# Half of a step's value products issued ahead of the second head's transposes, in grouped and latent attention

## The reference

```python
def sink_attend(q, segments, sink):          # grouped: 16 query heads of 64, 4 key heads, window 128
    s = jnp.einsum('bqhgd,bkhd->bhgqk', q, k) * WIN_SCALE      # masked outside the window
    p = jax.nn.softmax(jnp.concatenate(scores + [sink_col], axis=-1), axis=-1)
    outs.append(jnp.einsum('bhgqk,bkhd->bqhgd', p[..., start:start + n], v))

def mla_attend(q_nope, q_rope, k_nope, k_rope, v):             # latent: 8 heads of 128 + 64
    s = (jnp.einsum('bqhd,bkhd->bhqk', q_nope, k_nope) + jnp.einsum('bqhr,bkr->bhqk', q_rope, k_rope)) * MLA_SCALE
    p = jax.nn.softmax(s, axis=-1)
    return jnp.einsum('bhqk,bkhd->bqhd', p, v)
```

## Time and profile before

| | us |
|---|---|
| runs of the kernel before | 2820.78, 2811.59, 2815.4; median 2815.4 |
| profiled execution, its own time | 2812.94 |
| its span, first to last instruction | 2811.3 |
| PE busy | 2719.0 (97%) |
| DVE, ACT, POOL busy | 1747.4 (62%), 1250.4 (44%), 232.2 (8%) |
| grouped attention, layer 0 | 785 to 949 of the span |
| latent attention, layer 0 | 1070 to 1161 |
| grouped attention, layer 1 | 2301 to 2393 |
| latent attention, layer 1 | 2485 to 2530 |
| PE's granted clock over the span | 0.99 of full speed |

### The profile page before, as it was taken

One profiled execution on the slowest core, in us unless ns is written; L12 is line 12 of the kernel. 1 busy time (PEld: TensorE's weight loads), 2 busy tenths in 40 slices (PEclk: granted clock), 3 DMA queues, 4 the chain that ended last, 5 costly groups with the idle time before them and its releaser, 6 DMA issues.

```text
span 2811.3 us, 42833 instructions
## 1 busy us (share of the span) xinstructions
PE 2719.0 (97%) x15754; PEld 2282.3 (81%) x15754; DVE 1747.4 (62%) x2898; ACT 1250.4 (44%) x2228; POOL 232.2 (8%) x318
## 2 busy tenths in 40 slices
PE   8999999999899999999999999999999989998998
PEld 6888898876666776788888898888988677877998
DVE  7777376656755443367676386773777776636764
ACT  3222354336555434445223363223553566554444
POOL 0000010110100000010000000000102110001000
PEclk9999999999999999999999999999999999999999
DMA  7555366420111221145554455553665222414654
GB/s 280 181 200 182 93 178 227 136 90 31 53 38 46 68 88 37 60 157 184 167 188 155 128 175 175 198 183 94 179 197 186 84 76 76 143 58 150 238 172 136
DMA packets 106596, 385.49 MB, mean 137 GB/s; under 512 B 11985, under 2 KB 13281, under 8 KB 104529
## 3 DMA queue, kind: packets, MB, share of 16 engines
q1 hardware_dynamic: 86018, 303.34, 33.4%
q0 software_dynamic: 20432, 80.18, 8.7%
HBM read 379.27 MB, written 4.20 MB: 136 GB/s over the span
## 4 chain that ended last, share of the span: by engine, by line
PE 86%; DVE 8%; ACT 3%; issue 2%; DMA 1%; POOL 0%; SPq 0%; POOLq 0%; DVEq 0%; ACTq 0%
PE ps L1982 24%; PE ps L1983 23%; PE ps L1990 23%; PE ps L921 3%; PE ps L900 3%; PE ps L883 2%; DVE wlo L1494 2%; PE ps L2046 1%; PE ps L2048 1%; PE ps L2043 1%; PE ps L873 1%; DVE mx L771 1%; ACT prob L687 1%; PE ps L1922 1%; PE ps L879 1%
## 5 line engine op out<-in xcount | busy, mean ns | idle before, releaser
L1494 DVE TENSOR_TENSOR wlo<-raw,whi 128x1024 fp32r<-128x1024 f32 x572 | 698.0, 1228 | 436.2 <-ACT whi L1181 435.5
L1982 PE MATMUL ps<-xhi,whi 128*128 128x512 f32 (+1 forms) x2432 | 823.9, 353 | 9.7 <-DVE xlo L1685 9.6
L1181 ACT ACTIVATE whi<-raw 128x1024 fp32r<-128x1024 f32 x572 | 604.8, 1058 | 487.9 <-PE ps L1990 443.6
L1983 PE MATMUL ps<-xlo,whi 128*128 128x512 f32 (+1 forms) x2432 | 815.4, 349 | 0.0
L1982 PEld LDWEIGHTS ps<-xhi,whi 128*128 128x128 f32 x2432 | 464.2, 191 | 75.5 <-issue 8.8
L1983 PEld LDWEIGHTS ps<-xlo,whi 128*128 128x128 f32 x2432 | 464.5, 191 | 57.3
L1990 PE MATMUL ps<-xhi,wlo 128*128 128x512 f32 (+1 forms) x2432 | 506.8, 351 | 1.6 <-DVE wlo L1494 1.6
L1990 PEld LDWEIGHTS ps<-xhi,wlo 128*128 128x128 f32 x2432 | 400.9, 191 | 59.5 <-DVE wlo L1494 2.3
L1752 DVE SCALAR_TENSOR_TENSOR work<-ada,work 128x1024 f32<-128x1024 f32 x256 | 299.8, 1221 | 4.6 <-DMA ada<-in_ada_rows 4.6
L1982 PE MATMUL ps<-ghi,whi 128*128 128x256 f32 (+1 forms) x968 | 279.4, 314 | 1.9 <-ACT whi L1181 1.9
L1983 PE MATMUL ps<-glo,whi 128*128 128x256 f32 (+1 forms) x968 | 278.6, 315 | 0.0
(11 more groups left out here) (217 smaller groups left out, 3295.6 us busy)
## 6 DMA issues: line engine op xcount, KB each, us to landing
raw<-in_ffn_in SPq DMA_DIRECT2D x192, 512.0 KB, 4.8
ada<-in_ada_rows POOLq DMA_DIRECT2D x128, 512.0 KB, 4.4
raw<-in_merge SPq DMA_DIRECT2D x96, 512.0 KB, 3.6
raw<-in_ffn_out SPq DMA_DIRECT2D x88, 512.0 KB, 3.6
raw<-in_ffn_out SPq DMA_DIRECT2D x44, 384.0 KB, 3.2
raw<-in_v_a SPq DMA_DIRECT2D x32, 512.0 KB, 4.4
raw<-in_qk_a SPq DMA_DIRECT2D x32, 512.0 KB, 3.7
raw<-in_wo SPq DMA_DIRECT2D x24, 512.0 KB, 4.2
```

The costliest lines, as they stand in the source:

```text
L1181: act.activation(whi[:, g.ring(SPLIT), :], raw[:, g.ring(RAW), :], ACT.Copy).then_inc(hi_ready, 1)
L1494: dve.tensor_tensor(wlo[:, g.ring(SPLIT), :], raw[:, g.ring(RAW), :], whi[:, g.ring(SPLIT), :].bitcast(F32), ALU.subtract).then_inc(lo_rea ...
L1982: pe.matmul(o, w, hi[:, first + c, ph.span], start=start, stop=False)
L1983: pe.matmul(o, w, lo[:, first + c, ph.span], start=False, stop=False)
```

## The change

`weighted` gets an argument `part`, which takes the first or the second half of the unit's list of products, and only the second bumps the semaphore `pv`. In `b` a half is half of the key blocks with both heads, in `c` it is one head. In the second slot of a step, the first half now stands between the scores and the second head's transposes, the second half behind them. The first step has no products, and the last unit's are whole as before.

```diff
@@ -900,7 +900,7 @@
-            def weighted(u):
+            def weighted(u, part=None):
                 b, kc0 = units[u][0], first_key(ph, u)
                 pe.wait_ge(done["pt"], base(ph, "pt") + many * (u + 1))
                 if u % ph.per_block == 0:
@@ -909,6 +909,8 @@
                 pieces = [(n, kc) for n in range(many) for kc in range(kc0, T // P)]
                 if ph.mode == "b":
                     pieces = [(n, kc) for kc in range(kc0, T // P) for n in range(many)]
+                if part is not None:
+                    pieces = pieces[part * len(pieces) // 2:(part + 1) * len(pieces) // 2]
                 for n, kc in pieces:
@@ -919,7 +921,8 @@
                         last = pe.matmul(ps[rows, OUT, to:to + P], a, w, start=kc == kc0, stop=kc == T // P - 1)
-                last.then_inc(done["pv"], 1)
+                if part != 0:
+                    last.then_inc(done["pv"], 1)
@@ -942,9 +945,13 @@
                 yield
                 if s + 3 < len(units):
                     scores(s + 3)
-                if many == 2 and s < len(units):
+                if many == 2 and 1 <= s < len(units):
+                    weighted(s - 1, 0)
                     turn(s, 1)
-                if 1 <= s <= len(units):
+                    weighted(s - 1, 1)
+                elif many == 2 and s == 0:
+                    turn(s, 1)
+                elif 1 <= s <= len(units):
                     weighted(s - 1)
```

## The result

The changed kernel takes **2827.28 us**, the median of 6 runs (2822.88 to 2827.94), against 2813.82 (2811.59 to 2820.78, 6 runs) for the kernel before on the same chip: ratio 1.0041, 95% interval 1.0029 to 1.0052. By that ratio it is slower by 11.5 us (8 to 15); the two medians differ by 13.5. The profiled execution took 2827.14 us, its span 2825.5. All lines of `weighted` are L923 in it, the half weight group is L1997.

The account below looks back on a forecast made before the run. PE, with work in 97% of the span, was taken as the bound; cuts 6.9, entries 2.8, latent cuts 0.5 and new waits 4.8 less gain 6.0 made +9.0 us, 2824.4 on the median of 2815.4; range 2816 to 2833.

Parts of the forecast that it names:

- Cuts: Grouped stages: cutting a unit's value products in two costs 0.15 us each, 46 units, 6.9 us.
- Entries: Grouped stages: going from scores or masks into value products costs 0.09 us, about 31 times, 2.8 us.
- New waits: First transposes of the next step wait for the copy that half the products no longer cover: 4.8 us, latent 0.5 included.
- Gain: All four stages: waits before the second head's transposes filled by half the products, 6.0 us, of which latent 1.5.
- Latent: Latent stages of both layers: 22 cuts cost 0.5 us, new waits 0.5, waits gone give 1.5.
- idle before the second transposes: Grouped stages, outside the first step: PE's idle there falls from about 7 to 4 us.
- Entries are free: Value products behind scores do not pay the fixed part again: +1.6 us, 2817; chance 0.25.
- Every change of mode pays in full: Mask-to-product changes cost 0.2 us, half-row scores into products the fixed 0.16 again: +14.6 us, 2830; chance 0.15.
- ACT falls behind: Grouped steps: exponentials queued behind the later second copy delay the next step's transposes, 5.5 us more, 2830; chance 0.10.
- All waits gone: No cost of cuts, no new wait, every second-head wait after the first step ended: about -9 us, 2806; chance 0.05.

Follow-up runs that it names:

- second series: The changed kernel once more, no edit, against the kernel before: 2824.5 us, median of 12, ratio 1.0028 (1.0017 to 1.0039).
- full-width kernels: Grouped value matmuls take all 128 columns (that part of the computation changed), in the kernel before and in the changed one: 2831.4 and 2837.4 us, one run each.

## Why the prediction was right

The forecast was 2824.4 us, +9.0; measured are 2827.3 with a ratio worth 8 to 15 us, in a second series 5 to 11 us, and +8.5 in the stages. The mechanism is the one that was forecast. That the sum came out within half a us of the stages is in part luck, for costs and gains were both set too low:

- **Cuts, 0.15 x 46 = 6.9 us**: each block length came out as worked out, 0.59 and 0.37. The full-width kernels show the cause.
- **Entries, 31 x 0.09 = 2.8**: right to the hundredth at the masks, and right that score products on half the rows pay nothing new. The count was off: 26 of the cut grouped steps have masks in front, 14 half-row scores, and 6 no scores. Missed were the 0.03 us more that transposes take behind value products. By block lengths (32 x 0.28 + 14 x 0.15) cuts and entries come to about 11 us in the grouped stages, where I had 9.7.
- **New waits, 4.8**: their sizes came out (0.26 by starts for four tiles behind 8 records, 0.48 behind 4). Their idle rose by 2.1 + 0.8 us in the grouped stages where I had said 2 to about 6: part of each such wait lies under the modelled ends of the records and is no idle time, some 0.07 us apiece, and one old wait of 0.55 shrank to 0.20.
- **Gain, 6.0**: the term that was most undersized. In the grouped stages, where it was 4.5, the costs of about 11 and new waits of about 4, against +9.0 in the stages, leave about 6. The two waits of 1.37 us shrank to 0.71, by 0.66 each and not by the 0.37 + 0.15 that I gave them, and the third of 0.71 went nearly whole. These are waits for ACT, and ACT is ready a fixed time after the scores before: the second of them ended 4.08 us after the mask products of the step before it in the kernel before (922.99 to 927.07) and 4.09 us after them in the changed one (934.08 to 938.17). All that PE does more since then counts as cover, the extra price of the cuts too. Layer 0 therefore grew by 5.0 us and not by 6.
- **Latent, +0.5 +0.5 -1.5**: -0.5 as measured, but by two errors that cancel. The window of the earlier trace rows ended 10 us before the stage of layer 0 did and left out the wait of 0.83 us at 1161.75. By starts the waits that went gave about 2.4 us (1.9 in layer 0), so cuts and new waits cost about 1.9. In layer 1 the half W had to wait for the output copy, which I had seen only in the grouped stage.
- The idle before the second transposes of the grouped stages fell further than from 7 to 4, from 6.5 to 1.6 us, because of the larger cover.

**The rivals.** "Entries are free" falls: first halves of 8 records behind the scores take 0.59, not under 0.5. "Every change of mode pays in full", with the prices that I gave it, falls too: at the masks 0.09 and not 0.2, on half rows nothing on top. Here the rule of the Trainium skill, "TensorEngine Tiling (Array Packing)", Key Properties, that changing the tiling mode drains the engine, has to be read with care. The rule names no price; the +14.6 us took prices from the rows. The traces agree with it in kind: the step between two records grows from 0.11 to 0.20 us where the mode changes, and the cost goes when the products are made full-width. But a block of half-row score products in front had its price already, to whatever followed. What one more cut costs is the number of changes that it adds, not the number that surround it: behind masks, where a cut adds two, 0.28 us, and behind half-row scores, where it adds one, 0.15. "ACT falls behind" did not come: no wait before the second transposes grew, and the new ones before the first have the length of a copy. "All waits gone" did not come either.

What I had put at the border of what can be told turned out just clear of it, and not by better knowledge: the first series gives +11.5 us, 3 us of it beyond the stages, which the spread of the clock from run to run can make.

## What to carry to other kernels

Filling a wait with half of a block costs what the block pays for starting and ending; read that from two lengths of the same block, before cutting it. And ask what the second half was covering: the cover taken from one wait is missing at the next. Where something else covers the next wait anyway, a block that pays for its borders is better moved whole, and only there. Here that turned +8.5 us into -7.5, with the full-width products of the latent stages still cut in half. And end the window of a wait table where the stage ends: one wait missed here hid an error elsewhere.

## What the runs showed of the hardware

Value products on 64 columns, two heads side by side, carry a fixed 0.15 to 0.16 us per uninterrupted block next to full-array work, and those on 128 columns none (in front of a weight group 16 records 1.70 us, 8 records 0.81). Entering them costs 0.09 us behind fp32r products or masks and nothing more behind products on 64 rows. In single records, a step from full-array work to 64-column products or back takes 0.20 us, where one without such a change takes 0.10 to 0.11.

The clock before and in the grouped stage of layer 0 goes with how the program began. With 13.7 us at 1.2 GHz near its start, the grouped stage of layer 0 began at full clock, in six profiles of six; with 17.1 or 20.5 us it had 6.8 us at 1.2 GHz near its beginning, in seven of seven. That, not the order of PE, moves this stage by 2.7 us between executions of one kernel (170.8 and 173.6 before the change, 175.9 and 178.6 with it). Why the start differs was not tried.
